# A hybrid projection with its single-column products between the wide steps

## The reference

```
p = h @ w_in                                   # latent: all columns
pc_kv = hc @ w_in[:, :KV_COLS]                 # context: keys, values, gates only
k = l2_norm(silu(dwconv(k part))); q likewise  # DeltaNet, per head of 128
q_lat, k_lat = rope(rms_norm(q part)), rope(rms_norm(k part))   # attention, per head of 64
mod = split(silu(c) @ mod_w[layer] + mod_b[layer], 6)           # shift, scale, gate vectors
```

## Time and profile before

| | |
|---|---|
| median of three runs | 1667.69 us (1678.2, 1667.43, 1667.69) |
| profiled execution, first to last instruction | 1674.9 us |
| its own time | not listed apart; the slowest run lies 3.3 us above the span |
| TensorE busy | 1569.7 us, 94% |
| weight loads | 1278.5 us, 76% |
| VectorE, ScalarE, GpSimd busy | 892.0, 668.5, 291.1 us |
| mean granted TensorE clock | 0.954 |

### The profile page before, as it was taken

The page is one execution under the profiler, slowest core; times in us unless marked ns, Lnnn a source line. Parts: engine busy times, 40 slices in busy tenths (PEclk is TensorE's granted clock), DMA queues, the critical chain, the costliest instruction groups (busy, mean ns, idle before and its releaser), DMA issues.

```text
span 1674.9 us, 19524 instructions
## 1 busy us (share of the span) xinstructions
PE 1569.7 (94%) x7778; PEld 1278.5 (76%) x7778; DVE 892.0 (53%) x1203; ACT 668.5 (40%) x1044; POOL 291.1 (17%) x206
## 2 busy tenths in 40 slices
PE   8899896689998899999999999999999999999997
PEld 2688786578975567788888888778887788888886
DVE  2645523876557775765554434475676644444222
ACT  2443536301227673354433322255532443443221
POOL 3028602334623342200000002000012000000000
PEclk9899899679999899999999999999998999999999
DMA  9325600000021215224422222346522222332221
GB/s 345 102 88 176 176 23 16 1 1 1 1 76 58 94 51 151 76 76 151 144 85 97 95 92 91 101 151 201 176 76 74 78 91 87 98 100 94 92 91 51
DMA packets 153909, 160.20 MB, mean 96 GB/s; under 512 B 11383, under 2 KB 151144, under 8 KB 152808
## 3 DMA queue, kind: packets, MB, share of 16 engines
q1 hardware_dynamic: 153344, 158.95, 29.7%
q10 hardware_dynamic: 488, 0.18, 0.0%
HBM read 157.03 MB, written 2.10 MB: 95 GB/s over the span
## 4 chain that ended last, share of the span: by engine, by line
PE 79%; DVE 11%; ACT 4%; POOL 3%; issue 2%; DMA 0%; SPq 0%; DVEq 0%; ACTq 0%; POOLq 0%
PE ps L559 18%; PE ps L560 18%; PE ps L561 18%; POOL mod_raw_e L2283 2%; DVE sub_prod L1826 1%; DVE blocks_inv L1829 1%; PE ps L1026 1%; PE ps L617 1%; PE ps L952 1%; PE ps L980 1%; PE ps L1007 1%; PE ps L1027 1%; PE ps L1028 1%; DVE w_lo L1617 1%; PE ps L675 1%
## 5 line engine op out<-in xcount | busy, mean ns | idle before, releaser
L1617 DVE TENSOR_TENSOR w_lo<-w_raw,w_hi 128x2048 fp32r<-128x2048 f32 x100 | 233.7, 2337 | 456.7 <-ACT w_hi L1255 456.7
L559 PE MATMUL ps<-h_hi,w_hi 128*128 128x512 f32 x968 | 380.3, 393 | 2.2 <-DVE w_lo L1617 2.2
L560 PE MATMUL ps<-h_lo,w_hi 128*128 128x512 f32 x968 | 379.0, 392 | 0.0
L561 PE MATMUL ps<-h_hi,w_lo 128*128 128x512 f32 x968 | 378.8, 391 | 0.0
L1255 ACT ACTIVATE w_hi<-w_raw 128x2048 fp32r<-128x2048 f32 x100 | 191.3, 1913 | 260.0 <-PE ps L561 225.2
L559 PEld LDWEIGHTS ps<-h_hi,w_hi 128*128 128x128 f32 x968 | 183.3, 189 | 40.7 <-DVE w_lo L1617 2.7
L561 PEld LDWEIGHTS ps<-h_hi,w_lo 128*128 128x128 f32 x968 | 183.1, 189 | 38.6
L560 PEld LDWEIGHTS ps<-h_lo,w_hi 128*128 128x128 f32 x968 | 183.4, 189 | 37.7
L559 PE MATMUL ps<-mid_hi,w_hi 128*128 128x512 f32 x338 | 133.8, 396 | 0.0
L561 PE MATMUL ps<-mid_hi,w_lo 128*128 128x512 f32 x338 | 132.4, 392 | 0.0
L560 PE MATMUL ps<-mid_lo,w_hi 128*128 128x512 f32 x338 | 132.2, 391 | 0.0
(11 more groups left out here) (360 smaller groups left out, 2751.7 us busy)
## 6 DMA issues: line engine op xcount, KB each, us to landing
w_raw<-in_ffn_w_up SPq DMA_DIRECT2D x44, 1024.0 KB, 5.1
w_raw<-in_ffn_w_down SPq DMA_DIRECT2D x16, 896.0 KB, 4.7
mod_raw_e<-in_mod_w SPq DMA_DIRECT2D x12, 1024.0 KB, 5.3
w_raw<-in_sc_w_in SPq DMA_DIRECT2D x12, 1024.0 KB, 5.2
mod_raw_c<-in_mod_w SPq DMA_DIRECT2D x11, 1024.0 KB, 5.2
mod_raw_s<-in_mod_w SPq DMA_DIRECT2D x11, 1024.0 KB, 7.8
w_raw<-in_hyb_w_in SPq DMA_DIRECT2D x9, 1024.0 KB, 7.8
mod_raw_a<-in_mod_w SPq DMA_DIRECT2D x8, 1024.0 KB, 16.0
```

What stands on the lines that cost most here:

```text
L559: mm(dst, hi, xh[:, k0 + k, :], start=first and k == 0, stop=False)
L560: mm(dst, hi, xl[:, k0 + k, :], start=False, stop=False)
L561: i = mm(dst, lo, xh[:, k0 + k, :], start=False, stop=last and k == nk - 1)
L1617: V.tensor_tensor(wlo[s][:, :], raw[s][:, :], f32(whi[s][:, :]), ALU.subtract).then_inc(sem("w_lo"), 1)
```

## The change

- `mm3` takes a generator, `between`, and moves it on by one before each step. `unit_columns(u)` yields after each single-column product: the columns of the modulation of unit u, then the items of `STATS_IN[u]`: 0 and 1 in unit 8, 2 in unit 9, 3 and 4 in unit 10, 5 and 6 in unit 11. So at most one product stands before each of the 16 steps on the latent tokens; what is left over follows the unit. A wait of a product now stands between steps.
- Item 7 is summed behind unit 11, after the wait for the last tile.
- The squares have three buffers instead of two, and a square waits for the item three before it. When ScalarE squares (`ITEMS_IN`) is not changed.
- The third buffer lies on the place of the rotary tables. Their loads wait for the third root (`nsd` 3), and the loads of unit 12 stand behind them.

```diff
-        sqt = [region(f"sqt{i}", ALL, 63 + 3 * i) for i in range(2)]
+        sqt = [region(f"sqt{i}", ALL, a0) for i, a0 in enumerate((63, 66, 58))]
+        STATS_IN = {8: (0, 1), 9: (2,), 10: (3, 4), 11: (5, 6)}
...
             sp.wait_ge(sem("tile"), 2 * U_WOUT)
-            sp.dma_start(cosT[:, :], A["cos"]).then_inc(sem("rope_in"), 16)
-            sp.dma_start(sinT[:, :], A["sin"]).then_inc(sem("rope_in"), 16)
             for u in range(U_WOUT - 2, U_WOUT + 2):
                 for j in early_at(u):
                     load_early(j)
+            sp.wait_ge(sem("nsd"), 3)
+            sp.dma_start(cosT[:, :], A["cos"]).then_inc(sem("rope_in"), 16)
+            sp.dma_start(sinT[:, :], A["sin"]).then_inc(sem("rope_in"), 16)
             load_wout(12)
...
-            def mm3(dst, cols, nk, xh, xl, s, k0=0, first=True, last=True):
+            def mm3(dst, cols, nk, xh, xl, s, k0=0, first=True, last=True, between=None):
                 for k in range(nk):
+                    if between:
+                        next(between, None)
                     hi, lo = cols(wh, k), cols(wl, k)
...
             def item_stat(e):
+                for _ in item_columns(e):
+                    pass
+
+            def item_columns(e):
                 g = item_group(e)
                 pe.wait_ge(sem("nsq"), e + 1)
...
                 for j in range(items[e][1] // P):
-                    i = mm(bank(ITEM_BANK[g], 1 if e < 8 else 2, item_col(e, j)), sqt[e % 2][:, j * P:(j + 1) * P],
+                    i = mm(bank(ITEM_BANK[g], 1 if e < 8 else 2, item_col(e, j)), sqt[e % 3][:, j * P:(j + 1) * P],
                            ones[:, 0:1] if e < 8 else const[:, C_BLK, 0:P:HD], start=True, stop=True)
-                i.then_inc(sem("nst"), 1)
+                    if j == items[e][1] // P - 1:
+                        i.then_inc(sem("nst"), 1)
+                    yield
+
+            def unit_columns(u):
+                for j in early_at(u - 3):
+                    pe.wait_ge(sem("mod_acc"), acc_c(j))
+                    for part in range(2):
+                        mod_column(7, 16 + 2 * j + part, macc[:, j % 6, part * P:(part + 1) * P])
+                        yield
+                for e in STATS_IN.get(u, ()):
+                    yield from item_columns(e)
...
+                small = unit_columns(u)
                 for r in range(tiles):
...
-                    i = mm3(bank(lat % 4), lambda w, k: cols(w, k, r), KC, h_hi, h_lo, s)
+                    i = mm3(bank(lat % 4), lambda w, k: cols(w, k, r), KC, h_hi, h_lo, s, between=small)
...
-                mod_columns(early_at(u - 3))
-                for e in ITEMS_IN.get(u - 1, ()):
-                    item_stat(e)
+                for _ in small:
+                    pass
...
             pe.wait_ge(sem("ev"), len(EVENTS))
+            item_stat(7)
             for e in ITEM_GROUPS[2]:
...
             def square(e):
                 t, n = items[e]
-                if e >= 2:
-                    act.wait_ge(sem("nst"), e - 1)
-                nc.scalar.activation(sqt[e % 2][:, 0:n], t, ACT.Square).then_inc(sem("nsq"), 1)
+                if e >= 3:
+                    act.wait_ge(sem("nst"), e - 2)
+                nc.scalar.activation(sqt[e % 3][:, 0:n], t, ACT.Square).then_inc(sem("nsq"), 1)
```

## The result

The changed kernel takes 1680.07 us (median of 10 runs, 1677.76 to 1681.11) against 1671.8 us of the kernel before (10 runs, 1667.43 to 1678.52). The ratio is 1.0047, 95% interval 1.0031 to 1.0063: **slower by 8.3 us**, half a per cent. The way was forecast, the size (3.5 us) was not, and 1680.07 lies outside the range. The forecast of 1671.2 stood on the three runs then shown, 1667.69; with ten runs the median of the same kernel is 1671.8. Of the miss of 8.9 us, 4.1 are that reference and 4.8 are the sum of the forecast: +3.5 us were forecast and +8.3 measured.

A forecast was written before the change was run, and what follows sets the result against it. Only some 65 us of the hybrid projection change, summed along TensorE's timeline: waits of 10.4 us and a cold stretch outweigh what is removed. Unit 11 ends at 249.7 against 246.2: +3.5 on 1667.7, 1671.2 us; range 1664.5 to 1677.

The forecast's parts named there:

- Wait of item 1: Middle of unit 8: TensorE waits 9.0 us, from 192.1 until the square of item 1 is ready at 201.1.
- Price of an interleaved product: Product between wide steps: 0.22 us, with ends 0.20 and 0.30; a step with a product takes 0.91 us.
- the edge of 0.10 us: Extra time at the wide product behind a run of small ones; if each interleaved product paid it, each would cost 0.30.
- Start of unit 8: Unit 8 starts on TensorE at 183.0, where it used to start at 189.5: 6.5 us won.
- rivals 2 and 3: First: item 1 doesn't hold TensorE, -2.5 us, 1665.2, 13%. Second: no new wait counts, -8.7 us, 1659.0, 7%.
- rival 3: Units 8 to 11: no new wait counts, only what is removed; -8.7 us, 1659.0 us, chance 7%.
- Nothing on the way to this square depends on what the change made early: Square of item 1 on ScalarE: keeps its old time, starting at 200.32 and ready at 201.1.
- Low clock behind the wait: Last six steps of unit 8: 3.4 us at the low clock, half lost, 1.7 us.
- From there on, term by term: TensorE's ends of units: unit 8 at 208.3, unit 9 at 221.5, unit 10 at 236.2, unit 11 at 249.7.
- The second wait: Unit 10, near 227: TensorE waits 1.4 us for the square of item 4, with no loss of clock counted.
- The bounds: Sum: +1.1 us with products at 0.20 and no cold stretch; +9.5 with dearer products and more time at low clock.
- Tail and tables: Behind unit 11: copy wait and item 7 take 1.7 us as before; rotary tables land at 262.6, hidden by 0.7 us.

The follow-up runs named there:

- early squares: Changed kernel with the squares of items 1 and 2 made at the end of ScalarE's section for unit 6: 1670.82 us, ratio 0.9979.
- one entry of the table: Changed kernel with item 1 summed in unit 9 instead of unit 8, ScalarE's order untouched: 1672.33 us, ratio 0.9992.
- placed products: Early squares kernel, with item 2 ahead of the modulation's columns in unit 9 and unit 10's items from its fourth step: 1667.92 us, ratio 0.9968.
- columns only: Kernel before with only the modulation's 24 products between the steps; statistics, two buffers and tables as before: 1674.19 us, ratio 1.0001.

## Why the prediction was right in its way and wrong in its size

- **Wait of item 1, place and cause:** right. Idle 9.29 us, forecast 9.0; the early squares take it away, one entry of the table takes it away.
- **Price of an interleaved product:** right. 0.92 us for the step, forecast 0.91; at the full clock a product shows 0.23 us, so the edge of 0.10 us, which would have made it 0.30, isn't there.
- **Start of unit 8:** 184.2, forecast 183.0. I had taken the split of unit 8 as the last thing that it waits for and left out the bank that VectorE has to free. Hidden in the wait here, but in rivals 2 and 3 it wasn't: unit 9 couldn't have started at 197.6 in either of them; its earliest start in any run is 200.12. The kernel with placed products came to 5.7 us under the one before, between the two; the price of rival 3 was out of reach for this reason.
- **"Nothing on the way to this square depends on what the change made early": this is the step that failed.** Its square was ready at 204.4, forecast 201.1: 3.3 us. VectorE's split of unit 9 took 4.34 us. In the profile of before the same split took 2.6 us, with its convolution ending about 199.7. The split began 1.6 us later, and then GpSimd was first: it started its pair of wide adds at 195.96, VectorE at 196.11, so VectorE stood behind it. In the profile of before it was the other way round: VectorE's split began at 194.48, and GpSimd's sum at 195.11 took 2.60 us instead of 0.73 and let its pair begin only at 197.67. Holding GpSimd back gives a split of 2.29 us and a square 1.8 us earlier. The Trainium skill ("SBUF — State Buffer", "SBUF: two separate sides") says that the two engines share a port pair, that whoever starts first, GpSimd or a VectorE instruction with two inputs in SBUF, has it for the whole instruction, and that the other blocks. The rows agree: 0.15 us later, 4.34 us; 0.03 us earlier, 2.29 us. The other 1.6 us are the later landing of the load (9.5 us against 8.0), and they also are what lost VectorE its lead. Why the load lands later is open, and so is the first cause of the 3.3 us.
- **Low clock behind the wait:** mis-sized. I took 1.7 us from the earlier trace rows. From the square (204.4) to the end of unit 8 (212.7) are 8.3 us; six steps at 0.92 are 5.5, so 2.8 us were lost, 1.1 more than forecast. With the wait filled, 5.9 us instead of 8.45 to the next split, 2.6 us. The bound I gave for it, 1.7 and 1.6 more, held.
- **From there on, term by term right:** end of unit 8 212.7 (forecast 208.3), start of the gate sums 240.8 (236.2), copy behind unit 11 254.4 (249.7 and the latency). The lag of 4.4 us behind the forecast stays about the same (4.6 and 4.5): 3.3 from the square and 1.1 from the clock. The second wait is 1.28 us, forecast 1.4, and left the clock alone as I had taken.
- **The bounds:** the stage came to +8.0 us, inside my +1.1 to +9.5. That is luck: 4.4 of the 6.0 us up to the upper end were dearer products and a cold stretch at the second wait, neither of which came, and a late square wasn't in it.
- **Tail and tables:** right. From the copy behind unit 11 to `dn_ready` 16.9 us, before 16.8. The last table lands at 270.3, 1.1 us before `dn_ready` ends at 271.5 (forecast 0.7 of room). The run with these two edits alone shows no difference. In six of the twelve profiles this stretch takes 18.3 to 18.4 us, with a granted clock of 0.57 to 0.77 in a window of 4 us ahead of `dn_ready`; one of them is columns only, which has the tables early, so the tables aren't what makes it. The rows at 247.92 are those of item 0; the prediction calls them item 8, which changes no number.
- **The reference:** three runs gave 1667.69, ten gave 1671.8. The kernel before scatters over 11 us, the changed one over 3.4. I had thought of the cold stretches of this stage, which fall differently from one execution to the next, but the two profiles at hand say otherwise: of the 5.9 us between the spans of the kernel before and of the one with buffer and tables alone, 1.5 lie before `dn_ready` and 4.4 behind it. What makes the scatter is open.

## What to carry to other kernels

A product that is moved between the steps of an in-order engine brings its wait with it, and everything behind it in the queue now waits too: before interleaving, write down when each input is ready, and give every product the first place behind that. Moving one entry of the table, or two squares, turned a loss of 8 us into none or a small gain. When work is started earlier, recompute the operations of the other engines that will now overlap, rather than carry their old durations over.

## What the runs showed of the hardware that was not expected

- A VectorE subtraction of 128x2048 took 2.29 us alone, 4.24 to 4.43 us when GpSimd had begun a wide add 0.08 to 0.26 us ahead of it (six profiles), and 2.29 us when it began 0.03 us before GpSimd. A VectorE product of the same size, in the run with buffer and tables alone, also took 2.29 us with a lead of 0.03 us.
- Behind 9.3 us of idle time TensorE ran at the lower of its two levels (granted clock 0.50) from 204.5 to about 209.8, 5.3 us. The stretches of the earlier trace rows are 3.1 us, behind 4.27 us of idle time and 18 small records, and 3.4 us, behind 32 small records without idle time. Twenty such records from 218.09 to 220.24 weren't followed by it, nor was the second wait of 1.28 us.
- A load of 1024 KB landed 7.9 to 8.0 us after issue with TensorE idle, 9.3 to 9.6 us in the kernels where unit 8 ran beside it. In the run where nothing was loaded behind it, the DMA engines had moved nearly all by 191.3, 2.1 us before it landed. That it depends on TensorE isn't shown.
